# Moving three orders in a hand-scheduled transformer kernel: softmax scaling, weight casts, and the last column of an output projection

## The reference, cut to what matters

```python
q = rms_norm(q) * gain * scale;  k = rms_norm(k) * gain          # 16 heads of 64
s_loc = q_row . k_window + bias;  s_ctx = q_row . k_ctx
p = softmax(concat(s_loc, s_ctx));  o = p_loc @ v_window + p_ctx @ v_ctx
x = x + g1 * (o @ w_o)
x = x + g2 * swiglu(rms_norm(x) * (1 + sc2) + sh2)
```

## Time and profile before

| | us |
|---|---|
| median of 3 runs | 3596.08 |
| the runs | 3594.61, 3596.08, 3603.01 |
| profiled execution, its own time | 3594.06 |
| its span, first to last instruction | 3592.3 |
| PE busy in the span | 3344.2 (93%) |
| DVE busy | 1735.6 (48%) |
| ACT busy | 1287.9 (36%) |
| POOL busy | 404.0 (11%) |
| chain that ended last: PE, DVE, ACT, POOL, issue | 79%, 8%, 5%, 4%, 3% |
| mean granted clock of PE | 0.973 |

### The profile page before, as it was taken

How to read it: one execution, slowest core, us unless ns; L and a number is a source line. 1 busy time by engine, 2 the same in 40 slices (tenths; PEclk the granted TensorE clock), 3 DMA queues, 4 the chain that set the end, 5 groups by cost and what they waited for, 6 DMA issues and landing times.

```text
span 3592.3 us, 42894 instructions
## 1 busy us (share of the span) xinstructions
PE 3344.2 (93%) x17064; PEld 2756.7 (77%) x17064; DVE 1735.6 (48%) x2595; ACT 1287.9 (36%) x1991; POOL 404.0 (11%) x400
## 2 busy tenths in 40 slices
PE   4999987999998999887999999999999999999898
PEld 3777766888887778776788878887768688877686
DVE  3666666755533676765533334343333333433333
ACT  2555543212123465563322333233332333333322
POOL 1111101000001253533000000001100000020000
PEclk7999998999999999998999999999999999999999
DMA  5222222665621211111333232222223222222132
GB/s 176 86 74 73 61 73 82 203 191 191 190 86 47 68 44 47 48 45 43 98 96 98 88 101 67 75 79 76 72 67 94 96 77 77 65 85 74 53 97 85
DMA packets 109286, 318.75 MB, mean 89 GB/s; under 512 B 28192, under 2 KB 30880, under 8 KB 108576
## 3 DMA queue, kind: packets, MB, share of 16 engines
q1 hardware_dynamic: 109088, 316.00, 28.1%
HBM read 313.86 MB, written 2.10 MB: 88 GB/s over the span
## 4 chain that ended last, share of the span: by engine, by line
PE 79%; DVE 8%; ACT 5%; POOL 4%; issue 3%; DMA 1%; SPq 0%; DVEq 0%; ACTq 0%; POOLq 0%
PE bank L1012 20%; PE bank L1014 19%; PE bank L1013 19%; PE bank L1017 3%; PE bank L1018 3%; PE bank L1019 3%; PE bank L1224 1%; PE bank L1098 1%; PE bank L1108 1%; DVE tmp L1691 1%; PE bank L1243 1%; PE bank L1253 1%; POOL hg_d L2134 1%; POOL hg_d L2133 1%; ACT L1281 1%
## 5 line engine op out<-in xcount | busy, mean ns | idle before, releaser
L1012 PE MATMUL bank<-h_high_lat,w_high 128*128 128x512 f32 x2742 | 1138.4, 415 | 100.9 <-DVE h_low_ctx L1697 35.7
L1639 DVE TENSOR_TENSOR w_low<-w_raw,w_high 128x1024 fp32r<-128x1024 f32 (+3 forms) x442 | 538.3, 1219 | 1165.7 <-ACT w_high L1301 1164.7
L1014 PE MATMUL bank<-h_high_lat,w_low 128*128 128x512 f32 x2742 | 1082.5, 395 | 0.0
L1013 PE MATMUL bank<-h_low_lat,w_high 128*128 128x512 f32 x2742 | 1082.0, 395 | 0.0
L1301 ACT CAST w_high<-w_raw 128x1024 fp32r<-128x1024 f32 (+3 forms) x442 | 451.6, 1023 | 1329.4 <-PE bank L1014 853.4
L1012 PEld LDWEIGHTS bank<-h_high_lat,w_high 128*128 128x128 f32 x2742 | 522.4, 191 | 225.3 <-issue 82.9
L1014 PEld LDWEIGHTS bank<-h_high_lat,w_low 128*128 128x128 f32 x2742 | 522.3, 190 | 113.7
L1013 PEld LDWEIGHTS bank<-h_low_lat,w_high 128*128 128x128 f32 x2742 | 523.8, 191 | 78.8 <-issue 7.8
L2090 POOL TENSOR_TENSOR rstd<-rstd,square 128x512 f32<-128x512 f32 (+1 forms) x42 | 64.7, 1540 | 1480.0 <-ACT square L1282 1479.3
L1017 PE MATMUL bank<-h_high_ctx,w_high 128*128 128x256 f32 x795 | 225.4, 284 | 0.0
L1018 PE MATMUL bank<-h_low_ctx,w_high 128*128 128x256 f32 x795 | 225.3, 283 | 0.0
(11 more groups left out here) (260 smaller groups left out, 4406.2 us busy)
## 6 DMA issues: line engine op xcount, KB each, us to landing
w_raw<-in_w_in_dram SPq DMA_DIRECT2D x176, 512.0 KB, 3.5
w_raw<-in_ada_w_dram SPq DMA_DIRECT2D x88, 512.0 KB, 3.7
w_raw<-in_ffn_in_dram SPq DMA_DIRECT2D x88, 512.0 KB, 3.6
w_raw<-in_w_ada_dram SPq DMA_DIRECT2D x48, 512.0 KB, 4.4
w_raw<-in_hg_in_dram SPq DMA_DIRECT2D x40, 512.0 KB, 3.5
w_raw<-in_ffn_out_dram SPq DMA_DIRECT2D x32, 512.0 KB, 3.5
w_raw<-in_qkv_dram SPq DMA_DIRECT2D x24, 512.0 KB, 3.6
w_raw<-in_proj_ret_dram SPq DMA_DIRECT2D x16, 512.0 KB, 3.5
```

The source lines that it names most:

```text
L1012: e.matmul(lat_b, a, h[:, k, :], start=start, stop=False)
L1013: e.matmul(lat_b, a, l[:, k, :], start=False, stop=False)
L1014: done = e.matmul(lat_b, b, h[:, k, :], start=False, stop=stop)
L1639: e.tensor_tensor(w_lo[n % 2][:, 0:w], raw[slot][:, 0:w], w_hi[n % 2][:, 0:w].bitcast(F32), ALU.subtract).then_inc(s_lo, 1)
```

## The change

It has four edits, all in the order of events.

1. `na_nm` of a turn moves from phase 3 to phase 2 and ahead of that phase's `na_va`.
2. While the attention runs, `flush_rows` (L1657) moves from k == 4 to k == 5.
3. In `project_last`, closing product m follows group k = m of the sixth block, where it followed k = m + 2. The load and cast of the seventh block's weights, which stand behind closing product 4, move with it from k = 6 to k = 4.
4. At the end of `project_last`, `flush` comes before `preload(2)`.

```diff
-                if k == 4:
+                if k == 5:
                     self.flush_rows()
...
         def between(k):
-            m = k - 2
-            if 0 <= m < EARLY:
+            m = k
+            if m < EARLY:
                 self.ev("last", which, m, n)
                 self.feed(s, m)
             if m == EARLY - 1:
                 self.preload()
...
         for m in range(EARLY + 1, KC):
             self.piece(W[m], KC, rhs, ("res", m, layer, 2, s))
+        self.flush()
         self.preload(2)
-        self.flush()
...
                 if phase == 0 and turn < 5:
                     self.ev("na_sc", j, turn)
+                if phase == 2 and turn < 5:
+                    self.ev("na_nm", j, turn)
                 if phase == 2 and 1 <= turn <= 5:
                     self.ev("na_va", j, turn - 1)
-                if phase == 3 and turn < 5:
-                    self.ev("na_nm", j, turn)
```

## The result

| | before | changed | ratio, 95% interval |
|---|---|---|---|
| median of the first comparison, us | 3595.83 (4 runs) | 3548.51 (4 runs, 3545.68 to 3552.08) | 0.9865 [0.9848, 0.9882] |
| measured again, on one chip with two of the experiments, us | 3600.13 (9 runs) | 3547.72 (4 runs) | 0.9852 [0.9839, 0.9866] |
| profiled execution, its own time, us | 3594.06 | 3545.68 | |
| its span, us | 3592.3 | 3543.9 | |
| mean granted clock of PE | 0.973 | 0.976 | |

Faster by 47.3 us; 3552 was predicted, with 3543 to 3570 as the range.

A forecast was written before the change was run, and what follows sets the result against it. PE's waits were taken to bound the kernel. Attention 23.9, first projection 10.4 and second 8.0 us sum to 42.3 us off the profiled 3594.06, giving 3551.8; 3552 us was predicted, range 3543 to 3570.

The forecast's parts named there:

- The bound: Whole kernel: PE is busy 93% of the span, so the places where PE waits are what to remove.
- the slower rival: Attention: scaling stands in DVE's queue for its exponentials and delays everything behind it; 3616 us at 1.0 us a turn; chance 0.03.
- Edits 1 and 2, 23.9 us: Attention: 24.6 us saved by moving the scaling, less 0.7 us charged for the last head's context copy.
- Half of the 0.31 us inside the na_q group: Attention, na_q turn: eight transposes take 1.35 us instead of 1.04; half of that excess was counted as saved, 0.15 us.
- The charge of 0.7 us for the context copy: Last head: the context row now stands ahead of the context copy, costing between 0 and 1.2 us.
- its term: Attention: 22.3 us of transposes' waits for the scaling plus 2.3 us inside late groups of eight, together 24.6 us.
- the whole of 1.69 us goes: Attention, na_v piece: scaling fills DVE's hole before the value copy, so the transposes' 1.69 us wait disappears.
- Edit 3, 3.5 us: Projections, before the seventh block: two more groups cover the wait for weights, saving 2.1 and 1.4 us.
- I keep the 2.0 us: First projection: the seventh block's split, beside POOL's add, still costs 2.0 us; alone it would give 0.8 us more.
- The clock, 1.0 + 1.3 us: Projections, behind the seventh block's gap: shorter gaps lose less to half clock, saving 1.0 us in the first, 1.3 in the second.
- the clock stays up: Rival, projections: gaps of 2.0 and 2.2 us bring no clock fall, another 1.7 us saved each; 3548.4 us; chance 0.15.
- Edit 4, 7.3 + 5.3 us: Projections, eighth block's end to first feed-forward group: 17.2 us becomes 9.8 to 9.9, and 13.1 becomes 7.8.

The follow-up runs named there:

- two of the experiments: Changed kernel with the context row back at k == 4, 3549.83 us; changed kernel with late-turn scalings, weight cast and last head's context row moved, 3538.8 us.
- edit 1 alone: Kernel before with only the scaling moved to phase 2, ahead of that phase's value products: 3566.19 us, ratio 0.9908.
- a group taken away again: Changed kernel with m = k - 1 for m = k, two groups of cover before the seventh block instead of three: 3552.22 us, ratio 0.9877.
- the kernel with two exceptions to one rule for all turns: Changed kernel with the fifth turn's scaling one step earlier and the last pair's third turn's two steps earlier: 3537.37 us, ratio 0.9836.
- the one with every scaling right behind its scores: Changed kernel with the scaling in phase 0 instead of phase 2: 3545.65 us, ratio 0.986.
- edits 1 and 2: Kernel before with the scaling in phase 2 and the context row at k == 5, projections as before: 3568.41 us, ratio 0.9914.
- edit 4: Kernel before with only flush() moved ahead of preload(2) at the end of project_last: 3585.85 us, ratio 0.9962.
- all edits together: Changed kernel plus late-turn scalings earlier, seventh block's cast ahead of the square, last head's context row behind its context copy: 3538.8 us, ratio 0.9826.

## Why the prediction was right, point by point

**The bound.** Right. The waits of PE held the whole effect, and no other engine became one: DVE waited for exponentials in 16 of the 40 turns, 5.2 us in all, so the slower rival, which needed 0.5 us in each, did not come. The waits of DVE, after (total us, times, longest us):

```profile
DVE na_stat L1822 <- ACT na_p L1282: 5.2, 16, 0.6
```

**Edits 1 and 2, 23.9 us.** Right in the mechanism, and within 2 us in size. A pair of heads takes 46.24 us (the same group starts at 203.93 and at 250.17) where it took 49.72 (209.24 and 258.96): 3.5 us, as said. The transposes' wait fell to 2.5 us, where "under 2" was said; six of the seven left are the 0.18 us of the na_q turn (0.1 said), and the seventh was missed. Half of the 0.31 us inside the na_q group was taken as saved, but its eight transposes take 1.35 us as before; in its place the transposes one turn ahead of the na_v stall went from 1.22 us (at 238.09) to 1.04 (at 231.52), which the sum had not counted. In the last head the third turn meets the next piece's split, residual and modulation product ahead of its scaling, as in a na_v piece of the kernel before, but one step later (timeline, DVE and PE, changed kernel):

```profile
479.54 1.09 DVE L1639 TENSOR_TENSOR w_low<-w_raw,w_high 128x896 fp32r<-128x896 f32 x1 [1.73 <-ACT w_high L1301]
...
481.60 1.22 DVE L1650 SCALAR_TENSOR_TENSOR ada_product<-w_raw,c_rows 128x1024 f32<-128x1024 f32 x1
...
483.53 0.49 DVE L1826 TENSOR_SCALAR na_p<-na_p,na_stat 128x512 f32<-128x512 f32 x1
...
483.57 1.23 PE L1108 MATMUL bank<-matrices,na_p 128*128 128x128 f32 x8 [1.44 <-DVE na_p L1826]
```

1.44 us, for which the sum had no term. The charge of 0.7 us for the context copy measured 0.5 (2.45 to 2.96).

In the medians edit 1 alone gave more than its term (32.8 us against 24.6). A stall that sometimes brings a fall of the clock, which the one trace I read did not have, accounts for up to 4.7 us in a trace; the rest is open. So the step "the whole of 1.69 us goes" was right for that trace and too small for the median.

**Edit 3, 3.5 us.** The cover was right: 1.33 us less gap in the second projection (1.4 said), and a group taken away again gave 0.67 back. In the first the gap fell by 2.82 us and not 2.1. The step that failed is "I keep the 2.0 us" for the split behind POOL: the order of the two is a matter of 0.01 us, and in both traces of the changed kernel the split went through in 1.23 us; the sum had left that case out and priced it at 0.8 us more gain. The sum's way had no POOL in it either, and named DVE as what is late next; DVE had caught up, and it is POOL's row of adds that holds the last square (1.00 us of wait). The Trainium skill (SBUF — State Buffer, "SBUF: two separate sides") has a DVE instruction with two SBUF inputs and one of GpSimd that reads SBUF lock each other out for a whole instruction; here that holds both ways, 2.91 us for an add of 1.81 when the split goes first, 2.88 for a split of 1.23 when the add does.

**The clock, 1.0 + 1.3 us.** The second projection came as said: 1.29 us shorter from the seventh block to the end of the eighth (12.62 against 13.91). In the first no fall followed the 1.44 us gap, so 2.6 of the 2.7 us were saved, and 1.6 more at the sixth block, where I had left the fall in place; the kernel's second trace has that fall again. Between the projections another 2.2 us were saved and behind them 2.1 lost, neither by an edit. In this trace the rival "the clock stays up" holds for the first projection and not for the second (0.73 behind 2.06 us). Over all traces with these gaps, no fall came behind the 1.4 us of the first projection (five traces), and behind the 2.04 to 2.06 us of the second one came in the two of the changed kernel and in none of four others. So the 1.3 us of the second projection came out right partly by luck. The Trainium skill (TensorE: Matmul & The Clock Gate, "Why this matters for your kernels") sets the idle gap that costs the full clock higher than any of these; the runs do not agree with it: falls came behind single gaps of 1.70, 2.06 and 2.44 us, though not each time.

**Edit 4, 7.3 + 5.3 us.** Right, with 7.5 and 5.7 measured. From the eighth block's end 9.64 and 7.44 us (9.8 to 9.9 and 7.8 said). The casts do stand between the squares and rstd (546.11 for 1.97 us, rstd at 547.99), 4.18 us after PE's end, where 4.4 was worked out. Alone the edit took 8.0 us off the first projection from the seventh block on.

**The sum.** 42.3 us said, 48.4 in the profiled executions: 1.9 more in the attention, 4.1 more in the first projection, nearly all of it clock and the split's turn, 0.1 in the second, and 0.1 elsewhere.

## What to carry to other kernels

An operation that waits in an in-order queue should be put into the hole that its input leaves open, not at a regular distance: the kernel with two exceptions to one rule for all turns was 8.3 us shorter than the one with every scaling right behind its scores, in the same call, and some 10 us shorter than the one with two steps between, across calls. A stall of PE costs its length and sometimes a fall of the clock that the one trace at hand need not show (0, 2 and 3 falls in three traces with the same stalls), so take more than one trace of the kernel before. When gaps of a few us are taken out one after another, run the sum itself beside its parts: three more edits of some 10, 5 and 1 us, two of them measured in another call, gave 8.9 together, with 3.1 us lost in a stretch that none of them touches.

## What the runs showed of the hardware that was not expected

- DVE's split and POOL's add, started within 0.01 us of each other, run one after the other: the second stood for 1.1 us (POOL, 2.91 for 1.81) or 1.7 us (DVE, 2.88 for 1.23). Between the changed kernel and the same with edit 2 undone, 1.7 us of PE hang on which goes through: 1.44 against 3.12 us of gap.
- A fall of the granted clock is not set by the gap alone. Behind the same 2.45 us before the sixth block it came in six of the thirteen traces (the kernel before, edit 1, edits 1 and 2, edit 4, all edits together, and one of the two of the changed kernel) and not in the seven others; starts of 511.67 and 511.95 are on different sides. What decides between them stays open: no run varied only that.
- In the stretch behind the second projection, in which nothing was changed, the same instructions took 1884.7 us (edit 4 alone) to 1890.3 us (the scaling right behind its scores). PE ran at half clock for 48 us of it in the one and 64 in the other, and waited 57 and 62 us.
